# Odd layer: attention steps placed between the last projection tiles

## The reference, cut to what matters

```python
def heads(p):                                    # p = modulated tokens @ w_in
    qw, kw, vw, qn, kn, vn = jnp.split(p, splits, axis=-1)
    qw, kw = rms_norm(qw, ...), rms_norm(kw, ...)   # by head of 64
    qn, kn = rms_norm(qn, ...), rms_norm(kn, ...)
    return qw, kw, vw, qn, kn, vn
qwl, kwl = apply_axial_rope(qwl, cos, sin), apply_axial_rope(kwl, cos, sin)
ol = concatenate([
    window_attention(qwl, kwl, vwl, kwc, vwc, sink_win),      # 8 heads, 2 key/value heads, a sink
    neighbourhood_attention(qnl, knl, vnl, knc, vnc, rpb_na), # 8 heads, with a relative bias
]) @ w_out
```

## Time and profile before

| what | us |
|---|---|
| median of 3 runs | 1201.88 |
| profiled execution | 1201.33 |
| its span, first to last instruction | 1199.5 |
| TensorE busy | 1161.0 |
| VectorE busy | 840.7 |
| ScalarE busy | 617.4 |
| first matmul of the first output tile, after the span's start | 984.44 |

### The profile page before, as it was taken

How to read it: one execution, slowest core, us unless ns; L and a number is a source line. 1 busy time by engine, 2 the same in 40 slices (tenths; PEclk the granted TensorE clock), 3 DMA queues, 4 the chain that set the end, 5 groups by cost and what they waited for, 6 DMA issues and landing times.

```text
span 1199.5 us, 17207 instructions
## 1 busy us (share of the span) xinstructions
PE 1161.0 (97%) x6430; PEld 931.9 (78%) x6430; DVE 840.7 (70%) x1208; ACT 617.4 (51%) x1074; POOL 84.5 (7%) x73
## 2 busy tenths in 40 slices
PE   5999899999999999999999999999999999999998
PEld 3567677787777787887887887887887579998997
DVE  4563678888879556893883882897777977754655
ACT  5541384858675446621421421446855777654553
POOL 0000101010010033000000000034000004000000
PEclk9999999999999999999999999999999999999999
DMA  9857234242422232643543643632344004455554
GB/s 363 343 215 273 88 119 128 88 138 70 120 95 80 87 111 97 238 156 123 214 155 123 221 146 123 228 139 70 123 132 132 2 2 174 160 181 189 191 180 155
DMA packets 49893, 179.13 MB, mean 149 GB/s; under 512 B 5216, under 2 KB 7584, under 8 KB 47776
## 3 DMA queue, kind: packets, MB, share of 16 engines
q1 hardware_dynamic: 49536, 177.66, 42.9%
q10 hardware_dynamic: 288, 0.56, 0.2%
HBM read 177.05 MB, written 1.15 MB: 149 GB/s over the span
## 4 chain that ended last, share of the span: by engine, by line
PE 78%; DVE 8%; ACT 7%; DMA 3%; issue 2%; SPq 0%; DVEq 0%; ACTq 0%
PE ps L1916 50%; PE ps L1923 9%; PE ps L2210 6%; ACT ey L1256 3%; PE ps L2008 2%; DMA mhalf<-in_w_mod 1%; DVE sm L1864 1%; ACT ey L1259 1%; PE ps L1939 1%; ACT cacc L1204 1%; PE ps L2121 1%; DVE prob L1889 1%; DVE ycomb L1696 1%; PE ps L2328 1%; DMA xload<-in_ctx 1%
## 5 line engine op out<-in xcount | busy, mean ns | idle before, releaser
L1400 DVE TENSOR_TENSOR w_lo<-raw,w_hi 128x1024 fp32r<-128x1024 f32 x206 | 262.7, 1276 | 90.2 <-ACT w_hi L1030 90.1
L1030 ACT ACTIVATE w_hi<-raw 128x1024 fp32r<-128x1024 f32 x206 | 216.8, 1053 | 195.0 <-DMA raw<-in_w_ff 156.8
L1916 PE MATMUL ps<-a_hi,w_hi 128*128 128x512 f32 (+1 forms) x820 | 299.2, 365 | 0.0
L1916 PE MATMUL ps<-a_hi,w_lo 128*128 128x512 f32 (+1 forms) x820 | 288.9, 352 | 0.0
L1916 PE MATMUL ps<-a_lo,w_hi 128*128 128x512 f32 (+1 forms) x820 | 288.7, 352 | 0.0
L1916 PEld LDWEIGHTS ps<-a_hi,w_hi 128*128 128x128 f32 x820 | 155.1, 189 | 25.1 <-issue 2.7
L1916 PEld LDWEIGHTS ps<-a_lo,w_hi 128*128 128x128 f32 x820 | 155.1, 189 | 23.2 <-issue 1.0
L1916 PEld LDWEIGHTS ps<-a_hi,w_lo 128*128 128x128 f32 x820 | 155.0, 189 | 21.4
L1916 PE MATMUL ps<-b_hi,w_hi 128*128 128x512 f32 x304 | 119.2, 392 | 0.0
L1916 PE MATMUL ps<-b_lo,w_hi 128*128 128x512 f32 x304 | 118.4, 390 | 0.0
L1916 PE MATMUL ps<-b_hi,w_lo 128*128 128x512 f32 x304 | 118.3, 389 | 0.0
(11 more groups left out here) (289 smaller groups left out, 1763.9 us busy)
## 6 DMA issues: line engine op xcount, KB each, us to landing
raw<-in_w_ff SPq DMA_DIRECT2D x128, 512.0 KB, 3.5
mring<-in_w_mod SPq DMA_DIRECT2D x32, 768.0 KB, 5.1
raw<-in_w_in_even SPq DMA_DIRECT2D x36, 512.0 KB, 5.6
mring<-in_w_mod SPq DMA_DIRECT2D x16, 1024.0 KB, 6.9
ey<-acum_rows SPq DMA_DIRECT2D x32, 384.0 KB, 4.9
raw<-in_w_in_odd SPq DMA_DIRECT2D x18, 512.0 KB, 3.5
mhalf<-in_w_mod SPq DMA_DIRECT2D x16, 512.0 KB, 9.6
raw<-in_w_out_even SPq DMA_DIRECT2D x16, 512.0 KB, 3.5
```

Source lines behind the costliest of these rows:

```text
L1030: nc.scalar.activation(w_hi[:, u % RING, :, :], raw[:, u % RING, :, :], ACT.Copy).then_inc(hi_done, 1)
L1400: v.tensor_tensor(w_lo[:, u % RING, :, :], raw[:, u % RING, :, :], w_hi[:, u % RING, :, :].bitcast(F32), ALU.subtract).then_inc(lo_done, 1)
L1916: ins = mm(out_ap, w_[:, n % RING, k, :], (x_[k][:, 0:ntok] if type(x_) is list else x_[:, k, 0:ntok]), start=(k == 0 and j == 0), stop=(k ...
```

## The change

```diff
-       for kind, i in (q.split(".") for q in ("v.0 kw.0 kn.0 kn.1 v.1 qw.0 qw.1 v.2 qw.2 qw.3 kn.2 qn.0 qn.1 kn.3 qn.2 qn.3 v.3 v.4").split())]
+       for kind, i in (q.split(".") for q in ("v.0 kw.0 kn.0 kn.1 v.1 qw.0 qw.1 kn.2 qw.2 qw.3 kn.3 qn.0 v.2 qn.1 v.3 qn.2 v.4 qn.3").split())]
+FIRST_STEP, BESIDE = 11, 8
...
-    for n in range(len(ODD) + 3):
-        if n == len(ODD) - 1:
-            s.append(("S", 0))
+    def attend(j):
+
+        if j == BESIDE:
+            s.append(("S", j + 1))
+        if j < BESIDE:
+            order = [("S", j + 1), ("PT", j), ("max", j + 1), ("O", j - 1), ("exp", j + 1)]
+            if j >= 2 and j % 2 == 0:
+                order += [("ohi", j // 2 - 1), ("olo", j // 2 - 1)]
+        else:
+            order = [("S", j + 2), ("ohi", (j - 2) // 2), ("max", j + 1), ("scale", j), ("olo", (j - 2) // 2), ("exp", j + 1), ("PT", j), ("O", j - 1)]
+        for kind, i in order:
+            if kind in ("ohi", "olo"):
+                if j < BESIDE or j % 2 == 1:
+                    s.append((kind, i))
+            elif 0 <= i < len(ATTN):
+                s.append((kind, i))
+    for n in range(FIRST_STEP + len(ATTN) + 1):
+        j = n - FIRST_STEP
+        if 0 <= j < BESIDE:
+            s.append(("scale", j))
         if n < len(ODD):
             gemm(*ODD[n][:2])
...
+        norms = [("hnorm",) + o for o in behind(2) if o[0] != "v"]
+        turns = [("rot",) + o for o in behind(3) if o[0] in ("kw", "qw")]
+        stats = [("hstat",) + o for o in behind(1) if o[0] != "v"]
+        values = [("vtok", o[1]) for o in behind(1) if o[0] == "v"]
+        if j < 0:
+            s.extend(stats + norms + turns + values)
+            for q in range(2):
+                s.extend(("dup", q) for o in behind(6 + q) if o[0] == "kw")
+            if j == -1:
+                attend(j)
+        else:
+            s.extend(turns)
+            attend(j)
+            s.extend(stats + norms + values)
...
-            job(st, B_AUX[n_aux % 2], freed=("hv_done", nk))
+            job(st, B_AUX[n_aux % 2 if st[1:] != ("kn", 3) and st[1] != "qn" else 1], freed=("hv_done", nk))
...
-                job(st + (par,), (B_SEG, B_GEMM[0])[st[1] % 2] + par)
+                job(st + (par,), (B_SEG, B_GEMM[0])[st[1] % 2 if st[1] > BESIDE else 0] + par)
...
-            job(("Opair", t), (B_Y, B_AUX[1])[t % 2], freed=("split_done", 5 * KT + t + 1), filled=("pv_done", 4 * t + 4))
+            job(("Opair", t), B_AUX[1] if t >= 4 and t % 2 == 0 else B_Y, freed=("split_done", 5 * KT + t + 1), filled=("pv_done", 4 * t + 4))
...
-        prob = place("prob", [P, 3, 2, T], offset=region + 32768)
-        pT = place("pT", [P, 2, 2, T], offset=region + 32768 + 12288)
+        prob = place("prob", [P, 3, 2, T], offset=macc_at + 7680)
+        pT = place("pT", [P, 2, 2, T], offset=vtok_end)
+        o_hi = place("o_hi", [P, 4, SEQ], F32R, offset=hr_at)
+        o_lo = place("o_lo", [P, 4, SEQ], F32R, offset=hr_at + 4 * 4 * SEQ)
...
-                        pe.wait_ge(rope_done, len(rot_n))
-                    if t == 4:
-                        pe.wait_ge(qn_done, len(hn_n))
+                    if qt == 0 and t < 4:
+                        pe.wait_ge(rope_done, rot_n[("rot", "qw", t)] + 1)
+                    if qt == 0 and t >= 4:
+                        pe.wait_ge(qn_done, hn_n[("hnorm", "qn", t - 4)] + 1)
...
-                    if i == 0:
-                        pe.wait_ge(vtok_done, 5)
+                    if qt == 0:
+                        pe.wait_ge(vtok_done, 1 if t < 4 else t - 2)
```

More of the change, by code:

```diff
@@ L301, in script @@
+    for n in range(FIRST_STEP + len(ATTN) + 1):
+        j = n - FIRST_STEP
+        if 0 <= j < BESIDE:
+            s.append(("scale", j))
         if n < len(ODD):
             gemm(*ODD[n][:2])
-        if n == len(ODD) - 1:
-            s.append(("max", 0))
         behind = lambda back: [o[:2] for i, o in enumerate(ODD) if max(i, 1) == n - back]
-        for back, stage in ((1, "hstat"), (2, "hnorm"), (3, "rot")):
-            s.extend((stage,) + o for o in behind(back) if o[0] != "v" and (stage != "rot" or o[0][1] == "w"))
@@ L309, in script @@
[L309 to L319, removed]
@@ L320, in script @@
-    s += [("ohi", n // 2 - 1), ("olo", n // 2 - 1)]
+        norms = [("hnorm",) + o for o in behind(2) if o[0] != "v"]
[12 more added lines that the diff above has]
+            s.extend(stats + norms + values)
@@ L321, in script @@
+    s += [("ohi", len(ATTN) // 2 - 1), ("olo", len(ATTN) // 2 - 1)]
     s += [("grow",), ("vprep", NORM_FF1)]
@@ L624, in trunk @@
         vtok = place("vtok", [P, NCH, 5 * P])
+        vtok_end = at[0]
         at[0] = max(at[0], region + 2 * 16384)
@@ L632, in trunk @@
         bias = place("bias", [P, 2, 8, SEQ], offset=region + 16384)
-        prob = place("prob", [P, 3, 2, T], offset=region + 32768)
-        pT = place("pT", [P, 2, 2, T], offset=region + 32768 + 12288)
+        prob = place("prob", [P, 3, 2, T], offset=macc_at + 7680)
+        pT = place("pT", [P, 2, 2, T], offset=vtok_end)
+        assert vtok_end + 8 * 2 * T <= region + 16384
+        o_hi = place("o_hi", [P, 4, SEQ], F32R, offset=hr_at)
+        o_lo = place("o_lo", [P, 4, SEQ], F32R, offset=hr_at + 4 * 4 * SEQ)
         fin = place("fin", [P, 2, D], offset=out_at)
@@ L661, in trunk @@
         mix_hi = [mixE[:, 0, k, :] if k < 2 else a_hi[:, k, :] for k in range(KT)], [b_hi[:, k, :] for k in range(KT)]
+        attn_hi = [o_hi[:, k, :] if k < 4 else a_hi[:, k, 0:SEQ] for k in range(KT)]
+        attn_lo = [o_lo[:, k, :] if k < 4 else a_lo[:, k, 0:SEQ] for k in range(KT)]
         mix_lo = [mixE[:, 1, k, :] if k < 2 else a_lo[:, k, :] for k in range(KT)], [b_lo[:, k, :] for k in range(KT)]
@@ L736, in operands @@
                 return mix_hi[half], mix_lo[half]
+            if st[1] == "outO":
+                return attn_hi, attn_lo
             return a_hi, a_lo
@@ L1388, in _ @@
                     act.wait_ge(*filled(("Opair", st[1])))
-                    nc.scalar.activation(a_hi[:, st[1], 0:SEQ], ps[:, b, 0:SEQ], ACT.Copy).then_inc(signal(ohi_done), 1)
+                    nc.scalar.activation(attn_hi[st[1]], ps[:, b, 0:SEQ], ACT.Copy).then_inc(signal(ohi_done), 1)
         @block.vector
@@ L1893, in _ @@
                     b, _ = jobs[("Opair", t)]
-                    v.tensor_tensor(a_lo[:, t, 0:SEQ], ps[:, b, 0:SEQ], a_hi[:, t, 0:SEQ].bitcast(F32), ALU.subtract).then_inc(signal(split_done), 1)
+                    v.tensor_tensor(attn_lo[t], ps[:, b, 0:SEQ], attn_hi[t].bitcast(F32), ALU.subtract).then_inc(signal(split_done), 1)
                 elif k == "out":
```

## The result

The changed kernel takes 1214.66 us, the median of four runs (1214.19 to 1216.76), against 1201.56 for the kernel before (1201.00 to 1204.81). The ratio is 1.0105, with a 95% interval of 1.0093 to 1.0118: slower by about 13 us. The profiled execution took 1214.74 with a span of 1213.0. The forecast was 1208.7 with a range up to 1212: the direction was right, the size was 6.0 us short, and the time lies outside the range.

The account below looks back on a forecast made before the run. VectorE's queue was taken to pace the attention stage after the last tile, with TensorE's work nearly as long. 1201.33 + 5.7 for a later first output tile + 1.7 for the clock = 1208.7 us, range 1203 to 1212.

Parts of the forecast that it names:

- t = 0: End of kn.3, put at 890.60: 891.37 less the 0.77 that the second duplication no longer waits for a bank.
- S.1's wait: Second attention step's scores, beside the tiles: TensorE waits 0.5 us for the first exponentials to release the score banks.
- The statistics of kn.3: Early in the overlap: TensorE waits from 7.5 to 11.8 for bank 7, held until the norm of qw.3, +4.3 us.
- The statistics of qn.0: Next slot, after tile v.2: TensorE waits again for bank 7, until the norm of kn.3, +1.65 us.
- The five slots: Slots three to seven beside projection tiles: they cost nothing beyond TensorE's work and end at t = 61.2.
- PT.7: First probability transposes after the last tile: put at t = 65.9, or 956.5, within 1.5 us of its old place.
- The refill: After the last projection tile, PT.7 to scale.9: 10.8 us instead of 5.7, +5.1.
- Behind scale.9: End of the attention stage, up to the first output tile: both kernels alike, 22.86 us.
- The clock: TensorE's granted clock falls once after the 4.3 us wait, exposed during v.2: +1.7 us, ends 0 and 3.4.
- the first output tile: Sign at the end of the attention stage: it starts 6 to 8 us later, with nothing changed after it.
- clockless 990.2: Start of the first output tile without the clock term: 990.2 against 984.44 before, +5.7 us.
- rival (c): Attention stage: the waits come and the clock falls more than once, 1.7 to 3.4 more, 1210.4 to 1212; chance 0.15.

Follow-up runs that it names:

- f2_fill5all: The changed kernel plus unread matmuls, five ahead of the statistics of kn.3 and others in the four gaps after the last projection tile: 1209.88 us, ratio 1.0063.
- e1_bank: The changed kernel with the statistics of kn.3 put in the bank that the tile qn.0 has left: 1210.51 us, ratio 1.0075.
- e2_fill: The changed kernel plus nine unread matmuls just ahead of the wait at the statistics of kn.3: 1214.10 us, ratio 1.0105.
- f1_fill5: The changed kernel plus five unread matmuls just ahead of the wait at the statistics of kn.3: 1211.45 us, ratio 1.0078.
- h1_13: The changed kernel with attention begun two slots later, scores in double banks from S.6 on and first norms ahead of their attention steps: 1202.85 us, ratio 1.0008.
- i1_early: The kernel before, without the overlap, with S.1 and exp.0 listed ahead of the last value transposes: 1200.02 us, ratio 0.9988.
- e4_norms: The changed kernel with each slot's head norms listed ahead of the attention step instead of behind it: 1212.65 us, ratio 1.0092.
- h3_11: The changed kernel's start, with the refill of h1_13 and head norms ahead of the attention step in slots up to v.4: 1207.47 us, ratio 1.0042.
- g1_later: The changed kernel with attention begun two slots later and the statistics of kn.3 back in the alternating bank: 1207.9 us, ratio 1.0055.
- h6_11fill: h3_11 plus five unread matmuls ahead of the statistics of kn.3: 1206.71 us, ratio 1.0039.

## Why the prediction was wrong in size

Point by point, with t counted from the end of kn.3:

- *t = 0*: forecast 890.60, measured 891.00, +0.4. The wait of the duplication is gone as said. Of this 0.23 is what this execution was behind some 75 us earlier already. The other 0.17 is what is left when a statistics product of 0.86, which now stands where transposes of 0.45 stood, is set against a gap that gave back more than the 0.77.
- *S.1's wait*: 0.5 forecast, 0.43 measured.
- *The statistics of kn.3*: t = 11.8 forecast, 12.16 measured (903.16), a wait of 4.43 for 4.3. The chain of scale.0, low half, rotation, max.1 and norm was right in every link; scale.0 was 0.3 late.
- *The statistics of qn.0*: 1.65 forecast, 1.73 measured.
- *The five slots*: no wait, as forecast. PT.7 was put at t = 65.9. From the statistics product to it were 65.9 - 11.8 = 54.1; f2_fill5all, with the clock kept, has 55.35. So 1.2 were missing (apart from a slip: the durations of the five slots add up to t = 61.1, not 61.2, and no later term uses it), 0.3 of it ahead of the statistics of qn.0 and 0.9 in small distances behind them.
- *The refill*: 10.8 forecast from PT.7 to scale.9, 10.9 with the clock kept.
- *Behind scale.9*: 22.86, as forecast.
- ***The clock*: this is the step that failed.** The prediction said "I take 1.7, one fall exposed", and took for it the size of the one fall that the trace showed, 3.4 us at half speed. There were two falls, and each was low for 6.8 us. They cost 2.9 and 2.7, together 5.6 (f2_fill5all against after), 3.9 more than the 1.7. Two of the signs that the prediction named failed with it: PT.7 stood 5.55 behind its old place (forecast: within 1.5), and the first output tile 13.5 later (forecast: 6 to 8).

The sum: 0.4 for the start, 0.36 for the first statistics product, 2.9 and 2.7 for the clock, 1.2 for the slots and 0.1 for the refill are 7.7 us over the clockless 990.2, and 997.92 - 990.2 = 7.7. Of these 1.7 was forecast.

The case that came true was rival (c), to which 0.15 was given, and its price, 1.7 to 3.4 more, was too low as well: it had the number of falls but the length of the old one. The prediction listed what was needed. It forecast two stretches with some 6 and 7 us of idle TensorE, wrote that the second is "twice that of the fall seen in the trace", and still counted one fall. A wait of 4.4 us in one piece is another case than the gaps of 1.33, 1.06 and 0.96 of that trace, which had no row for it, so its upper bound should have been open. The length couldn't be read from the waits alone either: behind the same two waits of the refill, 1.34 and 2.24, the clock was low for 6.8 us in the kernel after and for 3.4 in e1_bank, e2_fill and f1_fill5. The range's top of 1212 came from the one old length.

What the change was worth at best could be read beforehand, and was: TensorE was idle for 3.3 + 3.0 us and lost at most 1.7 to the clock. h1_13 shows that the overlap doesn't take even that: with the start and the refill mended it is level with the kernel before. Its own gaps (1.46 at S.1, 2.00 at PT.5, 1.77 at PT.7) sum to 5.2, nearly the idle time that it was to remove. i1_early gets 1.2 of it with two steps moved by one place.

## What to carry to other kernels

When a stage is moved beside another, its latency isn't gone: it is paid once where the pipeline fills and again where the cover ends, so list every product that TensorE holds in order behind a bank whose release is queued behind the new work, at both ends. Price the clock by the piece of idle time: for each forecast wait ask by itself whether the clock falls after it, and leave the bound open for more than the one length seen, since here equal waits were followed by low stretches of 3.4 and of 6.8 us. Before a large overlap is built, try to move the one step that stands behind an unrelated wait.

## What the runs showed of the hardware

- The stretches at the 1.2 GHz level in this stage lasted 3.4 or 6.8 us. It was 3.4 before (gaps of 1.33, 1.06 and 0.96), at waits of 2.03 in e1_bank, 2.38 and 3.57 in e4_norms, 2.37 in h3_11, 1.77 in h1_13 and 2.29 in g1_later, and in the refill of e1_bank, e2_fill and f1_fill5 (waits of 1.34 and 2.24). It was 6.8 at the 4.43 of the kernel after, at a wait of 3.92 in e4_norms, and at waits of 1.34 and 2.24 in the kernel after and in g1_later. There was no fall behind waits of 1.73, 2.09 and 1.74 in the kernel after, of 2.00 in h1_13, of 2.02 and 1.55 in h3_11, and of 0.84, 1.29 and 1.09 in i1_early. Why equal waits differ stays open; the runs weren't made to tell.
- A low stretch of 6.8 us cost 2.9 and 2.7 us of time, one of 3.4 us in the refill 1.6, and the one of before, under VectorE's queue, 0.3.
- Unread matmuls in a wait kept the clock at 1.00 behind that wait in all six kernels that had them, and gave back up to 2.9 us where their length fitted the wait. Where they were too long they took away what the clock gave: nothing was left in h6_11fill.
- A matmul of float32 operands over 512 columns leaves two records and takes 0.86 us. The 0.43 that I took at first is the distance of two records.
